# Two products in place of three in the stick-breaking scores, with keys and queries laid out over 128 rows

## What is computed

```python
z = jnp.einsum('bhqd,bhkd->bhqk', qblk, kh) * scale
strict = kpos[None, :] < qp[:, None]
log_keep = jnp.where(strict, jax.nn.log_sigmoid(-z), 0.0)
between = lax.cumsum(log_keep, axis=..., reverse=True) - log_keep
w = jnp.where(strict, jnp.exp(jax.nn.log_sigmoid(z) + between), 0.0)
out = jnp.einsum('bhqk,bhkd->bhqd', w, vh)
```

## Time and profile before

| | |
|---|---|
| median of 3 runs | 2719.13 us (2718.26 to 2719.65) |
| profiled execution | 2719.73 us |
| its span, first to last instruction | 2717.9 us |
| TensorE busy | 2694.4 us, 99% |
| VectorE busy | 1576.7 us, 58% |
| ScalarE busy | 1150.4 us, 42% |
| GpSimd busy | 625.6 us, 23% |
| mean granted TensorE clock | 0.998 |

### The profile page before, as it was taken

How to read it: one execution, slowest core, us unless ns; L and a number is a source line. 1 busy time by engine, 2 the same in 40 slices (tenths; PEclk the granted TensorE clock), 3 DMA queues, 4 the chain that set the end, 5 groups by cost and what they waited for, 6 DMA issues and landing times.

```text
span 2717.9 us, 31965 instructions
## 1 busy us (share of the span) xinstructions
PE 2694.4 (99%) x12918; PEld 2254.4 (83%) x12918; DVE 1576.7 (58%) x2307; ACT 1150.4 (42%) x1831; POOL 625.6 (23%) x401
## 2 busy tenths in 40 slices
PE   8999999999999999999999999999999999999999
PEld 7888888888888888888888888788888888788887
DVE  7556545344466646665575678744445668754444
ACT  4323323222347636533235767422224667522223
POOL 1000111011136525400004642411102452411100
PEclk9999999999999999999999999999999999999999
DMA  4232332332221222222322221233333221233332
GB/s 162 95 99 93 99 100 93 101 101 93 90 80 56 72 69 67 93 95 99 96 98 88 80 68 33 85 94 101 93 101 102 72 63 47 70 97 97 94 99 79
DMA packets 69412, 238.78 MB, mean 88 GB/s; under 512 B 7696, under 2 KB 10256, under 8 KB 69264
## 3 DMA queue, kind: packets, MB, share of 16 engines
q1 hardware_dynamic: 69264, 236.73, 27.6%
HBM read 234.60 MB, written 2.10 MB: 87 GB/s over the span
## 4 chain that ended last, share of the span: by engine, by line
PE 93%; DVE 3%; ACT 2%; POOL 1%; issue 0%; DMA 0%; SPq 0%; ACTq 0%; POOLq 0%
PE ps L414 30%; PE ps L416 29%; PE ps L415 29%; DVE ptl L1556 1%; PE ps L544 1%; PE ps L442 1%; ACT wh L932 0%; PE ps L767 0%; PE ps L766 0%; POOL acc L2336 0%; PE ps L604 0%; PE ps L605 0%; ACT pth L941 0%; DMA raw<-in_pool_in 0%; PE ps L466 0%
## 5 line engine op out<-in xcount | busy, mean ns | idle before, releaser
L932 ACT ACTIVATE wh<-raw 128x1024 fp32r<-128x1024 f32 (+2 forms) x453 | 465.0, 1028 | 741.7 <-PE ps L416 738.5
L414 PE MATMUL ps<-xh,wh 128*128 128x512 f32 x1920 | 753.5, 392 | 0.0
L416 PE MATMUL ps<-xh,wl 128*128 128x512 f32 x1920 | 747.5, 389 | 0.0
L415 PE MATMUL ps<-xl,wh 128*128 128x512 f32 x1920 | 747.3, 389 | 0.0
L1548 DVE TENSOR_TENSOR wl<-raw,wh 128x1024 fp32r<-128x1024 f32 (+1 forms) x339 | 449.4, 1326 | 151.2 <-ACT wh L932 151.0
L414 PE MATMUL ps<-yh,wh 128*128 128x512 f32 x1088 | 425.1, 391 | 2.6 <-ACT t L960 1.6
L414 PEld LDWEIGHTS ps<-xh,wh 128*128 128x128 f32 x1920 | 360.5, 188 | 76.4 <-issue 2.2
L415 PEld LDWEIGHTS ps<-xl,wh 128*128 128x128 f32 x1920 | 360.5, 188 | 76.0 <-issue 2.2
L415 PE MATMUL ps<-yl,wh 128*128 128x512 f32 x1088 | 423.5, 389 | 0.0
L416 PE MATMUL ps<-yh,wl 128*128 128x512 f32 x1088 | 423.4, 389 | 0.0
L416 PEld LDWEIGHTS ps<-xh,wl 128*128 128x128 f32 x1920 | 360.3, 188 | 75.2
(11 more groups left out here) (261 smaller groups left out, 3647.7 us busy)
## 6 DMA issues: line engine op xcount, KB each, us to landing
raw<-in_ff SPq DMA_DIRECT2D x120, 512.0 KB, 3.6
raw<-in_pool_in SPq DMA_DIRECT2D x64, 512.0 KB, 3.3
raw<-in_conv_in SPq DMA_DIRECT2D x64, 512.0 KB, 3.3
raw<-in_pool_out SPq DMA_DIRECT2D x32, 512.0 KB, 3.3
raw<-in_qk SPq DMA_DIRECT2D x32, 512.0 KB, 3.7
raw<-in_pool_grp SPq DMA_DIRECT2D x16, 512.0 KB, 3.3
raw<-in_conv_out SPq DMA_DIRECT2D x16, 512.0 KB, 3.3
raw<-in_mla_z SPq DMA_DIRECT2D x16, 512.0 KB, 3.6
```

Source lines behind the costliest of these rows:

```text
L414: pe.do.matmul(o, lh, rh_, start=start, stop=False)
L415: pe.do.matmul(o, lh, rl_, start=False, stop=False)
L416: return pe.do.matmul(o, ll, rh_, start=False, stop=stop)
L932: act.do.activation(h[:, 0:ncol], r[:, 0:ncol], ACT.Copy).then_inc(*mark("whi", ("whi", k)))
```

## The change

The key's high and low parts of one head now stand over each other in one tile of 128 rows: for e = 0 the high part in rows 0 to 63 and the low part in rows 64 to 127, for e = 1 the other way round. The head's high query stands in both halves of another tile. One product of 128 rows then gives high by high plus low by high, and one product of 64 rows (high key by low query) the rest: two products for each key block in place of three. ScalarE and VectorE each handle the keys in two instructions of 64 rows where there was one of 128. The high query of head 2p is copied into both halves of `qs[0]` by two DMAs on ScalarE's queue (128 KB each), that of head 2p + 1 stays in place and is copied over the upper half by a third (`double`), once the first two have landed. The covers of key blocks 2 and 3 become one product of 256 columns.

```diff
         def sqk(p):
-            return (YH[2], YL[2], YH[3], YL[3]) if p == 1 else G[8:12]
+            q0, ql_, k0, k1 = (YH[2], YL[2], YH[3], YL[3]) if p == 1 else G[8:12]
+            return (q0, (YL[1], YH[1], YH[2], YH[3])[p]), ql_, (k0, k1)
...
                 def sb_scores(h):
...
-                    q_h, q_l, k_h, k_l = sqk(p)
+                    qs, q_l, ks = sqk(p)
                     rr = slice(64 * e, 64 * e + 64)
                     pe.wait_ge(*at("pl", l, "sq", p))
-                    pe.wait_ge(*at("pl", l, "sk", p))
+                    pe.wait_ge(*at("plx", l, p) if e == 0 else at("pl", l, "sk", p))
+                    pe.wait_ge(*at("dup", l, p, e))
...
-                            mm3(o, k_h[rr, kc], k_l[rr, kc], q_h[rr, qc], q_l[rr, qc], kb == kbs[0], False)
+                            pe.do.matmul(o, ks[e][:, kc], qs[e][:, qc], start=kb == kbs[0], stop=False)
+                            pe.do.matmul(o, ks[e][rr, kc], q_l[rr, qc], start=False, stop=False)
                     for kbs, k0, width in GR:
                         b = ps("ss", l, h, kbs[0])
-                        for kb in kbs:
-                            o = b[:, KOFF[kb] - k0:KOFF[kb] - k0 + 128]
-                            mm = pe.do.matmul(o, identr[:, :], hidden[:, :], start=False, stop=kb == kbs[-1])
-                        mm.then_inc(*mark("group", ("mm", "ss", l, h, kbs[0])))
+                        o, cover = b[:, 0:128], hidden[:, :]
+                        if len(kbs) == 2:
+                            o = b[:, 0:512].rearrange("p (a c) -> p a c", a=2)[:, :, 0:128]
+                            cover = hidden[:, :].rearrange("p (a c) -> p a c", a=1).to_broadcast([128, 2, 128])
+                        pe.do.matmul(o, identr[:, :], cover, start=False, stop=True).then_inc(
+                            *mark("group", ("mm", "ss", l, h, kbs[0])))
...
                 def plain(nm, p):      # ScalarE
-                    dst = sqk(p)[0 if nm == "sq" else 2]
+                    qs, _, ks = sqk(p)
+                    t = temp("pj", l, nm, p)
                     if p > 1:
-                        act.wait_ge(*at("mm", "ss", l, 2 * p - 3 if p == 2 else 5, 0))
-                    high(dst[:, :], temp("pj", l, nm, p), ("pj", l, nm, p), ("plh", l, nm, p))
+                        act.wait_ge(*at("mm", "ss", l, 3 if p == 2 else 5, 0))
+                    if nm == "sk":
+                        high(ks[0][0:64, :], t[0:64, :], ("pj", l, nm, p), ("plhx", l, p))
+                        high(ks[1][64:128, :], t[64:128, :], ("pj", l, nm, p), ("plh", l, nm, p))
+                        return
+                    if p == 3:
+                        act.wait_ge(*at("mm", "ds", l, 2, 16))
+                    high(qs[1][:, :], t, ("pj", l, nm, p), ("plh", l, nm, p))
+                    act.wait_ge(*at("plh", l, nm, p))
+                    for rr in (slice(0, 64), slice(64, 128)):
+                        act.do.dma_start(f(qs[0][rr, :]), f(qs[1][0:64, :])).then_inc(*mark("dupa", ("dup", l, p, 0), by=16))
+
+                def double(p):
+                    q = sqk(p)[0][1]
+                    act.wait_ge(*at("dup", l, p, 0))
+                    act.wait_ge(*at("pl", l, "sq", p))
+                    if l or p:
+                        act.wait_ge(*at("dup", l, p - 1, 1) if p else at("dup", l - 1, 3, 1))
+                    act.do.dma_start(f(q[0:64, :]), f(q[64:128, :])).then_inc(*mark("dupb", ("dup", l, p, 1), by=16))
...
                 def plain(nm, k):      # VectorE
...
+                    if nm == "sk":
+                        low(ks[0][64:128, :], t[0:64, :], ks[0][0:64, :], ("plhx", l, k), ("plx", l, k))
+                        low(ks[1][0:64, :], t[64:128, :], ks[1][64:128, :], ("plh", l, nm, k), ("pl", l, nm, k),
+                            ("tfree", "pj", l, nm, k))
+                    else:
+                        low(q_l[:, :], t, qs[1][:, :], ("plh", l, nm, k), ("pl", l, nm, k), ("tfree", "pj", l, nm, k))
```

More of the change, by code:

```diff
@@ L71 @@
 SEMS = ("xin0", "xin1", "xin2", "xin3", "xin4", "xin5", "xin6", "xin7", "consts", "vec", "raw0", "raw1", "raw2", "raw3", "pos", "lam", "cos", "sin", "fn", "out",
-        "group", "whi", "wlo", "wlop", "act", "dve", "pool")
+        "group", "dupa", "dupb", "whi", "wlo", "wlop", "act", "dve", "pool")
 class Quiet:
@@ L108, in mark @@
         for r in results:
-            assert r not in self.value or r[0] in ("accfree", "wfree", "stored"), r
+            assert r not in self.value or r[0] in ("accfree", "wfree", "stored", "dup"), r
             self.value[r] = (name, self.total[name])
@@ L1356, in second_layer @@
                 soft(0)
+                double(0)
                 keep(0)
@@ L1371, in second_layer @@
                 keep(1)
+                double(1)
                 sb_out(0)
@@ L1418, in second_layer @@
                 df_exp(2, 34)
+                double(2)
                 weights_of(3)
@@ L1443, in second_layer @@
                 df_exp(3, 16)
+                double(3)
                 weights_of(5)
@@ L1991, in plain @@
                 def plain(nm, k):
-                    o = 0 if nm == "sq" else 2
-                    low(sqk(k)[o + 1][:, :], temp("pj", l, nm, k), sqk(k)[o][:, :],
-                        ("plh", l, nm, k), ("pl", l, nm, k), ("tfree", "pj", l, nm, k))
+                    qs, q_l, ks = sqk(k)
+                    t = temp("pj", l, nm, k)
+                    if nm == "sk":
[4 more added lines that the diff above has]
+                        low(q_l[:, :], t, qs[1][:, :], ("plh", l, nm, k), ("pl", l, nm, k), ("tfree", "pj", l, nm, k))
                 def turned(nm, h):
```

## The result

The changed kernel takes 2729.48 us (median of 6 runs, 2729.00 to 2730.47) against 2719.35 (median of 6, 2718.26 to 2719.65): 10.1 us more, ratio 1.0044, 95% interval 1.0034 to 1.0053. It is slower, as forecast, and inside the range; the forecast was 7.3 us more.

The account below looks back on a forecast made before the run. TensorE was taken as the bound, except for about 37 us a layer where the chain runs over ScalarE and VectorE. 2 x (2.35 + 1.3) = 7.3 us more gave 2726.4 us, range 2721 to 2733.

Parts of the forecast that it names:

- What a change of rows costs: In `sb_scores` on TensorE, each change between 128 and 64 rows costs 0.20 us; a head gets 0.40 us longer.
- heads 0 to 3: In TensorE's own stretch of each layer, the longer calls count in full: 4 x 0.40 = 1.60 us.
- The undrained array: Rival: TensorE does not drain between the new products, saving 0.71 us per head; 2714.6 us, or 2712.0; chance 0.09.
- Heads 5, 6, 7: Later calls of a layer: 0.35 us comes through for head 5, 0.40 for head 6; head 7's 0.40 is swallowed.
- Head 4 "is hidden": `sb_scores(4)` lies in the stretch of ScalarE and VectorE, which hides its longer call; priced at nothing.
- ScalarE: At pair 2, two DMA issues and the wait cost 0.9 us, the third issue 0.4; 1.3 us a layer, bounds 0 and 1.6.
- VectorE "nothing": The second low part of `sk` 2 fits a pause of 0.85 us; priced at nothing, upper bound 2 us a layer.
- The clock: Rival: the drop behind `sb_scores(7)` goes, 2723.0 us, chance 0.10; or another comes at a second place, 2729.8, chance 0.04.
- The copies: The DMA copies of the queries land in time, price nothing; if late, up to 2 us each at two places a layer.
- The sum: Two layers of 2.35 us for the calls and 1.3 for ScalarE: 7.3 us more, 2726.4 us.

Follow-up runs that it names:

- the grouped order: Changed kernel with each call's four products of 128 rows first, then the four of 64, then the covers: 2720.09 us, ratio 1.0011 to the kernel before.
- the form of 128 rows: Changed kernel with the second product of each key block over 128 rows too: 2718.28 us, ratio 1.0000 to the kernel before.
- all three moves: Changed kernel with `double(2)` behind `weights_of(3)`, second low half of `sk` 2 behind `plain("sq", 2)`, query 2's two DMA issues behind `df_turn(1)`: 2726.39 us, ratio 1.0030.
- TensorE's part alone: Kernel before with products of 128 and 64 rows per key block and the merged cover, without copies or halves: 2723.34 us, ratio 1.0023.

## Why the prediction was right, and by how much it was off

**What a change of rows costs.** Right, and shown: 0.31, 0.25, 0.37 and 0.43 us against the forecast 0.31, 0.26, 0.37 and 0.43; single changes in a row cost what the lone ones around the old calls did. A call takes 3.03 us, not 3.08 (the terms of the prediction add up to 3.06, and the last covers take 0.17, not 0.2), so heads 0 to 3 lose 0.33 each and not 0.40. The undrained array is ruled out by the starts, and the grouped order and the form of 128 rows show that the changes alone make the call long. The Trainium skill ("TensorEngine Tiling (Array Packing)", Key Properties) names the drain between tiling modes; the runs agree, and put 0.14 to 0.20 us on each change.

**Heads 5, 6, 7.** Right: 0.34 comes through for head 5 (0.35 forecast), 0.34 for head 6 (0.40), and head 7 is swallowed by its wait.

**Head 4 "is hidden".** Wrong, and with it the picture of the stretch. It was taken as ScalarE's and VectorE's until 1656. Once `sb_scores(4)` starts 4.5 us late, TensorE is the bound behind it, and its 0.65 us counts.

**ScalarE.** The two issues cost 1.2 us, not 0.9 (0.47 and 0.72 with the waits for the own copy and between). The third, priced at 0.4, costs nothing, since it stands behind what TensorE waits for; that it also waits for VectorE's low query had been overlooked. Moving it changed nothing.

**VectorE "nothing".** This is the mis-sized term. The second low half took 2.8 us, the pause of 0.85 took its part, and the upper bound of 2 us that the prediction named came through: the scaling of the next query starts 3.3 us later (1621.72 against 1618.42), of which the calls before make 1.3. Even scores wait for the first half only, but in VectorE's list the scaling of the next query stands behind the second. With the earlier trace rows at 2.88 us for the one instruction there, the same price for a second one beside it was the nearest row.

**The clock**, a rival at 0.10 and 0.04, happened in both ways at once: the drop of the earlier trace rows is gone and a longer one came earlier, 2.9 us lost against 1.6 given back. The 1.6 is against a run of the kernel before that had both its drops; not every run has. **The copies** landed in time in the changed kernel: issued at 1623.1 and 1623.6, they took 3.4 and 4.9 us and were wanted at 1630.6.

**The sum.** Forecast 3.65 us a layer: 2.35 for the calls, 1.3 for ScalarE. Measured 4.8 in the first layer: 2.0 for calls 0 to 3, 5 and 6, 0.65 for call 4, 3.2 for the waits, 1.3 net for the clock, less 2.35 of waits that the kernel had before and that the delay swallowed. So 2.0 of the 3.2 for the waits, the 0.65 and the 1.3 were not in the forecast, 4.0 us, and 2.35 of them were cancelled by a term that was not in it either. The calls (2.0 against 2.35) and ScalarE (1.2 against 1.3) were priced about right; that the total came as near as it did is in part luck.

## What to carry to other kernels

Before two products of TensorE are made of three, look at their numbers of rows: products of one kind are to stand together, and filling the short one up to 128 rows cost no time here (starts 0.11 and 0.23 us apart for 256 and 512 columns, as with 64 rows); whether the added term is harmless has to be seen case by case, here it is a product of two low parts. Where a chain over two engines hands over to TensorE, price each added instruction by the row of its neighbour at that very place, not by its mean, and look at what stands behind it in the list. And a delay that stands behind what TensorE waits for, like `double(2)` here, is worth nothing, neither when it is added nor when it is removed.

## What the runs showed of the hardware

A VectorE subtraction of 64 rows by 512 columns took 2.8 us twice while GpSimd made low weights, and 0.7 us where GpSimd did nothing. VectorE's timeline of the changed kernel:

```profile
1612.25 0.68 DVE L1583 TENSOR_TENSOR yl<-t,yh 128x512 fp32r<-128x512 f32 x1
...
1616.11 5.58 DVE L1583 TENSOR_TENSOR g<-t,g 64x512 fp32r<-64x512 f32 x2
```

The second of the two in the kernel with all three moves, where it stands behind the low query:

```profile
1627.73 0.69 DVE L1589 TENSOR_TENSOR g<-t,g 64x512 fp32r<-64x512 f32 x1
```

GpSimd's timeline of the changed kernel, over the same time:

```profile
1610.59 3.50 POOL L2375 TENSOR_TENSOR t<-t,sin 128x512 f32<-128x512 f32 x1
...
1615.48 8.43 POOL L2359 TENSOR_TENSOR wl<-raw,wh 128x1024 fp32r<-128x1024 f32 x3
```

The price is not a slower rate but a wait for GpSimd's instruction to end. GpSimd's three end at 1618.34, 1621.14 and 1623.92; the two subtractions end 0.55 us behind the first and the second, and so do all twelve of VectorE's subtractions of 512 columns from SBUF that take over 0.9 us in the first layer of the changed kernel, each behind the GpSimd instruction under which it began. So a second one that begins right under the next GpSimd instruction costs as much as the first. The other way round it is GpSimd that is held: its L2375 takes 3.50 us beside five subtractions of VectorE from 1610.11 to 1612.93, none of them over 0.7 us, and 1.30 at 1604.83. Scaling out of PSUM in the same time (L2013, 1621.72) took 0.69 us. The Trainium skill ("GPSIMD Engine Reference", Specifications) states that GpSimd shares its SBUF interfaces with VectorE, with contention for VectorE instructions of two SBUF inputs; this agrees with it.

A copy of 128 KB from SBUF to SBUF landed in 2.2 to 2.9 us in 19 of 24 cases in the changed kernel, and in 3.4 to 4.9 in the other five, each with weights of 512 KB under way beside it; with all three moves those of query 2 took up to 5.8.

The granted clock fell to 1.2 GHz for 3.4 or 6.8 us behind stretches with waits. It also fell without one: with TensorE's part alone at 1707.0, right behind `sb_scores(7)` with its changes of rows, though TensorE had been busy for 25.78 of the 25.80 us since `sb_scores(6)` began; with all three moves at 1705.8 in the same way. The changed kernel has the same call there and kept its clock. The profiled runs have none to four such stretches in the two layers, and the runs of one kernel differ in them: between the fastest and the slowest with TensorE's part alone lie 8.4 us, at mean granted clocks of 0.998 and 0.996. What exactly sets it off was not settled.
